# VectorE's order in the attention, two passes for the shared key, two transfers ahead of the experts, and unread products among the first turned rows, in one layer of a hybrid decoder

## What is computed

```
u = rmsnorm(h);  proj = u @ w_in        # c_q, c_kv, k_pe, hq, hf, hi, hg, gm, gh
o_mla = mla_branch(c_q, c_kv, k_pe)     # 8 heads, causal; k_pe: a rotary key of 32 columns, shared by all heads
o_hg  = hgrn2_branch(hq, hf, hi, hg)    # gated linear recurrence, chunkwise
merged = sigmoid(gm) * (o_mla @ w_br_mla) + sigmoid(gh) * (o_hg @ w_br_hgrn)
h = h + merged @ w_out
u = rmsnorm(h);  h = h + hier_moe(u)    # top group of 8, then top 2 of its 8 experts; 64 experts of width 256
return rmsnorm(h)[:, 16:]
```

## Time and profile before

| | us |
|---|---|
| median of 3 runs | 1494.26 |
| lowest and highest | 1493.94, 1495.15 |
| the profiled execution | 1496.1 |
| its span, first to last instruction | 1494.4 |
| TensorE busy | 1377.6 (92%) |
| VectorE, ScalarE busy | 581.8, 561.4 |
| mean granted TensorE clock | 0.980 |

### The profile page before, as it was taken

How to read it: one execution, slowest core, us unless ns; L and a number is a source line. 1 busy time by engine, 2 the same in 40 slices (tenths; PEclk the granted TensorE clock), 3 DMA queues, 4 the chain that set the end, 5 groups by cost and what they waited for, 6 DMA issues and landing times. The chain is left out here.

```text
span 1494.4 us, 21048 instructions
## 1 busy us (share of the span) xinstructions
PE 1377.6 (92%) x8471; PEld 983.6 (66%) x8471; DVE 581.8 (39%) x1303; ACT 561.4 (38%) x1066; POOL 101.6 (7%) x131
## 2 busy tenths in 40 slices
PE   5999999999999999999999999999987878688786
PEld 5888887787888887666667888855544444344442
DVE  6455565432531054656677556411110111111117
ACT  6534355222322146444552355533322222222223
POOL 0000000000000000000000011311111111111100
PEclk9999999999999999989999999999999999999998
DMA  6111111112234333112137654999999999999998
GB/s 185 43 29 43 29 29 43 30 32 78 80 97 122 101 89 124 57 36 71 36 120 240 253 194 157 321 416 415 415 416 416 416 417 416 416 416 417 415 403 333
DMA packets 130433, 312.53 MB, mean 209 GB/s; under 512 B 31120, under 2 KB 77200, under 8 KB 113184
## 3 DMA queue, kind: packets, MB, share of 16 engines
q1 hardware_dynamic: 118304, 285.96, 51.2%
q0 software_dynamic: 12032, 25.22, 4.4%
HBM read 283.81 MB, written 41.98 MB: 218 GB/s over the span
## 5 line engine op out<-in xcount | busy, mean ns | idle before, releaser
L2397 PE MATMUL ps<-r,m_xT 128*64 128x256 f32 x2048 | 253.4, 403 | 68.2 <-DMA r<-in_w 67.6
L130 PE MATMUL ps<-uTh,h_wh 128*128 128x512 f32 (+3 forms) x696 | 263.8, 379 | 4.4 <-DVE uTl L566 2.4
L131 PE MATMUL ps<-uTl,h_wh 128*128 128x512 f32 (+3 forms) x696 | 255.9, 368 | 0.0
L132 PE MATMUL ps<-uTh,h_wl 128*128 128x512 f32 (+3 forms) x696 | 255.6, 367 | 0.0
L2397 PEld LDWEIGHTS ps<-r,m_xT 128*64 128x64 f32 x2048 | 150.6, 145 | 153.5 <-DMA r<-in_w 76.1
L130 PEld LDWEIGHTS ps<-uTh,h_wh 128*128 128x128 f32 (+1 forms) x696 | 129.4, 186 | 28.7 <-DVE uTl L566 4.3
L2313 DVE TENSOR_TENSOR m_prod<-m_sig,ps 128x128 f32<-128x128 f32 x64 | 18.4, 288 | 333.4 <-ACT m_sig L2284 333.4
L132 PEld LDWEIGHTS ps<-uTh,h_wl 128*128 128x128 f32 (+1 forms) x696 | 129.3, 186 | 20.1
L131 PEld LDWEIGHTS ps<-uTl,h_wh 128*128 128x128 f32 (+1 forms) x696 | 129.6, 186 | 19.5 <-issue 0.2
L2379 PE MATMUL ps<-r,m_hT 128*64 128x512 f32 x512 | 122.4, 598 | 1.3 <-DVE m_hT L2317 0.9
L2274 ACT ACTIVATE m_y<-ps,gate 64x512 f32<-64x512 f32 x128 | 87.4, 682 | 80.0 <-PE ps L2379 78.4
(11 more groups left out here) (363 smaller groups left out, 2098.7 us busy)
## 6 DMA issues: line engine op xcount, KB each, us to landing
r<-in_w SPq DMA_DIRECT2D x190, 1024.0 KB, 24.3
h_w<-in_w_in SPq DMA_DIRECT2D x37, 512.0 KB, 4.3
gates<-h_sg POOLq DMA_DIRECT2D x16, 512.0 KB, 2.9
r<-y_moe SPq DMA_DIRECT2D x8, 1024.0 KB, 17.1
br_gate<-gates SPq DMA_DIRECT2D x14, 512.0 KB, 4.1
e_wo<-in_w_out SPq DMA_DIRECT2D x4, 1024.0 KB, 6.1
f_x<-in_x SPq DMA_DIRECT2D x8, 512.0 KB, 5.1
h_mid<-f_x SPq DMA_DIRECT2D x8, 512.0 KB, 4.5
```

Of the source, the lines that this page charges most:

```text
L130: pe.matmul(out, lh, rh, start=start, stop=False)
L131: pe.matmul(out, lh, rl, start=False, stop=False)
L132: return pe.matmul(out, ll, rh, start=False, stop=stop)
L2397: ins = pe.matmul(bank(UP_BANK + e % 2, 0, DE, CAP * f, CAP * (f + 1)).rearrange("p (r f) -> p r f", r=2), xT[i % 2][:, j, CAP * k:CAP * ( ...
```

## The change

- **Unread products.** A `keep_up` in the first stage puts 34 products of the identity with ones ahead of flip(0), then 6, 24 and 10 ahead of flips 1 to 3, and 12 behind flip(3), ahead of the first projection. They write bank 3, which nothing reads then.
- **Shared key.** The 32 columns of low weights are written beside the 32 of high weights, and a piece is 8 times two matmuls (high and low rows) with 64 weight columns in place of 8 times three with 32. Partitions 0 to 31 of the bank then hold the products with high weights, 32 to 63 those with low. ScalarE copies the first (counting `pp_ok`), VectorE adds the second (`summed_p`, counting `p_ok`).
- **Attention.** VectorE does peak(k+1,1) ahead of normed(k+1,0) in every step.
- **Transfers.** The last u is stored by ScalarE's queue, right behind its scaling and a wait for it, not by SyncE's; the first of expert 6's two upper transfers stands ahead of store_h(7) and of the wait for gathered rows.

```diff
@@ scalar, vector: the shared key
-                    act.activation(kpe[0:ROPE, c:c + m], bank(p % 3, 0, m, ROPE), ACT.Copy).then_inc(p_ok, 1)
+                    act.activation(kpe[0:ROPE, c:c + m], bank(p % 3, 0, m, ROPE), ACT.Copy).then_inc(pp_ok, 1)
...
-                dve.tensor_tensor(used(wl, J), used(w, J), used(wh, J).bitcast(F32), ALU.subtract).then_inc(wl_ok, 1)
+                low_part = wh[J % 2][:, :, ROPE:2 * ROPE] if JOBS[J][0] == "p" else used(wl, J)
+                dve.tensor_tensor(low_part, used(w, J), used(wh, J).bitcast(F32), ALU.subtract).then_inc(wl_ok, 1)
...
+            def summed_p(n):
+
+                c0, m = cols_of(LAT + 5)[n]
+                at_bank = spot[LAT + 5, n] % 3 * 512
+                dve.wait_ge(pp_ok, n + 1)
+                dve.tensor_tensor(kpe[0:ROPE, c0:c0 + m], kpe[0:ROPE, c0:c0 + m],
+                                  g.ps[ROPE:2 * ROPE, at_bank:at_bank + m], ALU.add).then_inc(p_ok, 1)
...
+                    if B == HG and s in (27, 29):
+                        summed_p(s // 2 - 13)
+            summed_p(2)
@@ tensor: the shared key
+                if JOBS[J][0] == "p":
+
+                    for j in range(4 * y, 4 * y + 4):
+                        for u_one in (g.uTh, g.uTl):
+                            last = pe.matmul(bank(p % 3, 0, m, 2 * ROPE), wh[J % 2][:, j, 0:2 * ROPE], u_one[:, j, col:col + m],
+                                             start=j == 0 and u_one is g.uTh, stop=j == DK - 1 and u_one is g.uTl)
+                for j in range(4 * y, 4 * y + 4) if JOBS[J][0] != "p" else ():
+                    last = mm3(pe, bank(p % 3, 0, m), wh[J % 2][:, j, :], wl[J % 2][:, j, :], g.uTh[:, j, col:col + m],
@@ tensor: the first turned rows
+            def keep_up(n):
+
+                for _ in range(n):
+                    pe.matmul(bank(RB, 0, P), g.ident[:, :], g.ones[:, :], start=True, stop=True)
+
             pe.wait_ge(consts, 4)
-            for n in range(4):
+            for n, unread in enumerate((34, 6, 24, 10)):
+                keep_up(unread)
                 flip(n)
+            keep_up(12)
@@ vector: the attention
-                if k + 2 == len(steps):
+                if more:
 
                     peak(k + 1, 1)
                     normed(k + 1, 0)
-                    normed(k + 1, 1)
-                elif more:
-                    normed(k + 1, 0)
-                    peak(k + 1, 1)
                     normed(k + 1, 1)
@@ sync and scalar: ahead of the experts
             sp.wait_ge(w_mm, 2 * TT)
-            store_u(TT - 1)
             g.load_down(sp, 4, 4)
             g.load_down(sp, 5, 5)
+            g.load_up(sp, 6, 6, (0,))
             store_h(TT - 1)
 
             sp.wait_ge(g.x_in[0], 16)
-            g.load_up(sp, 6, 6)
+            g.load_up(sp, 6, 6, (1,))
             g.load_down(sp, 6, 6)
...
                     act.activation(u[:, :], u[:, :], ACT.Copy, scale=sc[:, 14:15]).then_inc(u_ok, 1)
+                    act.wait_ge(u_ok, TT)
+                    act.dma_start(g.u2[t * P:(t + 1) * P, :], u[:, :]).then_inc(u_out, 16)
```

More of the change, by code:

```diff
@@ L211, in project_part @@
         sg_out = [sem(f"h_sg_out{b}") for b in range(2)]
+        pp_ok = sem("h_pp_ok")
         raw_ok, p_ok, ns_ok, ms_mm, nr_ok, n_ok, nh_ok, nl_ok = (
@@ L840, in half @@
                 col, m = cols_of(J)[n]
-                rows = ROPE if JOBS[J][0] == "p" else P
                 if cols_of(J) is REAL:
                     col += META
-                for j in range(4 * y, 4 * y + 4):
-                    last = mm3(pe, bank(p % 3, 0, m, rows), wh[J % 2][:, j, 0:rows], wl[J % 2][:, j, 0:rows], g.uTh[:, j, col:col + m],
+                if JOBS[J][0] == "p":
[5 more added lines that the diff above has]
+                    last = mm3(pe, bank(p % 3, 0, m), wh[J % 2][:, j, :], wl[J % 2][:, j, :], g.uTh[:, j, col:col + m],
                                g.uTl[:, j, col:col + m], j == 0, j == DK - 1)
@@ L1465, in expert_loaders, with load_up @@
     down = g.w2[0].rearrange("e (j p) n -> p e j n", j=2)
-    def load_up(eng, e, b):
-        for r in range(2):
+    def load_up(eng, e, b, parts=(0, 1)):
+        for r in parts:
             eng.dma_start(g.r13[b][:, r, :, :], up[r][:, bass.ds(e, 1), :, :].rearrange("p a j f -> p (a j) f")
```

## The result

| | before | changed | changed / before, 95% interval |
|---|---|---|---|
| median | 1494.66 | 1485.8 | 0.9941 (0.9923 to 0.996) |
| lowest and highest of 4 runs | 1493.94, 1495.15 | 1483.43, 1488.37 | |
| the profiled execution, its span | 1496.1, 1494.4 | 1488.4, 1486.6 | |

8.9 us are gone (6 to 11.5 by the interval of the ratio); 1486.2 was forecast. The sum held and two of its four terms did not: the attention gave 9 us where I had put 6, the transfers cost 2 us where I had put a gain of 1.5. That the sum still came out is luck: the errors cancel.

What follows compares the result with a forecast made beforehand. TensorE was taken to bound the kernel up to the routing, DMA in the experts. Unread products +3.2, shared key -3.8, attention -6.0 and transfers -1.5 sum to -8.1 us: from 1494.26 to 1486.2 us, range 1480.8 to 1493.6.

Steps and rivals of the forecast that it cites:

- The bound of each regime: Up to the routing TensorE sets the pace; in the experts the end follows DMA's bytes, and earlier savings pass on in full.
- Part 1: Start of the kernel: 86 unread calls delay the first projection to 26.1 us, less 1.4 for its warm clock: +3.2 us.
- the slow level ahead of the clock's rise: Kernel's start: work that begins slowly loses half the time until the clock rises, taken as 1.5 us.
- rival A: Unread products cost half or fit into existing waits, so the clock's gain stays: -2.8 in place of +3.2, 1480.2 us; chance 0.10.
- Part 2: Shared key: three pieces lose 8 matmuls each, 24 in all, and VectorE's additions lie in free slots: -3.8 us.
- Part 3: Attention: the new VectorE order removes most of TensorE's waits for normed rows: -6.0 us.
- all of them at best: Attention: of 8.3 us of waits 1.5 fall in the last step, so at most 6.8 us can be gained.
- head 0 pays 0.35: Attention: head 0's normed rows come later under the new order, so a stall of 0.35 us arises at turn(.,0).
- Part 4: Transfers around the routing: earlier loads close holes in DMA: -1.5 us, ends 0 and -3.
- the gain is 2.5 us less the gather's delay: Around the routing: a megabyte sent ahead gains 2.5 us less the gather's delay, which lies between 0 and 2.5.
- Rival B: Attention: TensorE waits for normed(.,0) in all steps, 7.0 us lost and no stall removed: 1499.2 us; chance 0.10.
- rival C: Stalls only move (-2.0 to -3.4), the gather is late (0), the clock slow to rise (+5.1): 1492.6 us; chance 0.15.

Runs made afterwards that it cites:

- e5: Changed kernel with SyncE storing u again ahead of the lower loads, expert 6's first upper megabyte still ahead: 1483.98 us, ratio 0.9925.
- e12: Same kernel as e10, but unread calls only ahead of the first two flips (17, 3, 0, 0 and none behind): 1479.22 us, ratio 0.9903.
- e4: Changed kernel with half the unread products, 43 calls (17, 3, 12, 5 and 6) in place of 86: 1477.94 us, ratio 0.9894.
- e7: Changed kernel with the old transfers put back and unread calls 20, 0, 9, 6 and 9: 1479.01 us, ratio 0.99.
- e2: Changed kernel without the 86 unread products: 1481.75 us, ratio 0.9909.
- e8: Kernel before with the shared key's two passes as the only change: 1490.15 us, ratio 0.9973.
- e3: Changed kernel with VectorE's old order in the attention: 1495.69 us, ratio 1.0002.
- e1: Changed kernel with the old transfers put back: SyncE stores u ahead of the lower loads, expert 6 behind the gathered rows: 1484.03 us, ratio 0.9928.
- e6: Changed kernel with expert 6 wholly behind the gathered rows, ScalarE still storing u: 1487.34 us, ratio 0.9955.
- e10: Changed kernel with half the unread products (17, 3, 12, 5 and 6 calls) and the old transfers put back: 1476.12 us, ratio 0.9878.
- e11: Same kernel as e10, but the lower loads of experts 4 and 5 (2 MB) moved behind the gathered rows: 1480.41 us, ratio 0.9912.

## Why the prediction was right, and where not

**The bound of each regime** held. What was gained ahead of the routing reached the last u (-10.4), and behind it the end followed DMA.

**Part 1, unread products: +3.2 said, +4.4 in the profile and +4.05 timed.** Two records a call at 0.112 us, 24.6 us for the sum of the calls and flips, TensorE as what is last, 1.4 us from the warm projection: all held. The mis-sized term is the slow level ahead of the clock's rise: I took 1.5 us and it was 27.37 - 24.6 = 2.8. It isn't a fixed price either: the row at 1.78 us is (10.38 - 0.27) - 67 x 0.112 = 2.6 us too long in the changed kernel and 2.2 in e5 with the same 34 calls, 2.7 in e12 and 1.9 in e4 with the same 17, and 1.5 in e7 with 20, always from the same start. What sets it stays open; the 1.5 us that I took is the lowest of them. The rule of the Trainium skill (TensorE: Matmul & The Clock Gate, section Why this matters for your kernels) to keep TensorE busy to get past the slow level isn't wrong for that: e4 gains 2 to 4 us by it over e2, the changed kernel loses 4 with twice the calls. What decides is whether the calls fit into the time in which nothing else is ready; rival A had the right place ("TensorE idles 8.49 us") and the wrong count.

**Part 2, shared key: -3.8 said, -3.8 and -3.9 (e8).**

**Part 3, attention: -6.0 said, -9.3 at equal clock.** The mechanism is as told. The step that failed is the bound "all of them at best", 6.8 us: I took the recorded idle time for all that a stall costs. (The bound was misread, too: 0.83 + 0.34 = 1.2 us of the 8.3 fall in the last step, not 1.5, so 7.1 were to be had.) Taking half of the low level's time off each, the new order gives 404.1 to 404.5 us from the sums to the merge in all ten profiled kernels that have it, the old order 413.3, 413.9 and 413.6 (before, e3, e8): 9.3 us (9.5 between kernels with equally many low stretches), while the recorded idle time fell by 8.3 - 1.2 = 7.1. About 0.2 us for each of ten stalls doesn't stand in the waits; block 3 shows 0.89 for 0.73. The rows of block 3 show where the rest is: idle is counted from the modelled end of the last matmul, and without a stall TensorE goes on before that end. In the changed kernel turn(.,1) starts 697.99 - 696.91 = 1.08 us after the scores, whose row lasts 1.25: an overlap of 0.17 us, and 0.73 + 0.17 is the 0.89, to a hundredth. For the other nine stalls this is argued by analogy. The step "head 0 pays 0.35" failed too: its turn(.,0) has no stall in any block but the last. And 1.7 us more of the profile's difference is the clock (1.4 with the 9.5 us), which was no term of the sum.

**Part 4, transfers: -1.5 said, +1.8 timed.** The failed step is "the gain is 2.5 us less the gather's delay". Three things are wrong in it. A megabyte sent ahead isn't gained where the buffers are full anyway: the hole moves to 970 us (e5 beside e1: to 968). The delay is not the gather's own (4.00 us, shorter than the 7.08 of the earlier trace rows) but that of the store that the gather waits for: u was written behind 3 MB of weights asked for 4 us before, 9.57 us in place of 5.2. And a queue of ScalarE's own is no way past them: the Trainium skill, DMA: Bandwidth & Descriptors, section Issuing engines are not separate DMA queues, says that transfers of all issuing engines interleave on the same 16 engines. I had cited it for "worth nothing" and not gone on to what it interleaves with; e6 agrees with it, at 8.37 us. In SyncE's list store_u stood ahead of the loads, and that order, I take it, was the protection; a store by SyncE behind the loads would have shown it.

**The sum.** +4.4 - 3.8 - 9.3 - 1.7 + 2.6 = -7.8 us, the difference of the spans. My -8.1 came out near it because its errors cancel: 1.2 too little for the unread products and 4.1 too much gain for the transfers stand against 3.3 too little gain in the attention and 1.7 of the clock (-8.1 + 1.2 + 4.1 - 3.3 - 1.7 = -7.8). By the medians the four parts are +4.05 (e2), -3.9 (e8), -9.9 (e3) and +1.8 us (e1), together -7.95 against -8.9 measured, within the intervals. Rival B's stalls and rival C's "stalls only move" are refuted by the waits and e3; C's late gather was true.

## To carry to other kernels

Unread products pay only in time in which the engine has nothing else to do: count them (records, at the slow pace until the clock is up) against the pause, part by part; 43 calls gained 2 to 4 us where 86 lost 4. A store that a gather waits for belongs ahead of the bulk loads in the order of asking (5.2 us against 8.4 to 9.6 behind them); whether the other queue had a part in it these runs don't say. And where an in-order engine stalls in mid-stream, a stall can be worth more than the waits show (here some 0.2 us each), so the recorded idle time is no upper bound of what its removal gives.

## What was not expected of the hardware

- In the attention the low level of the clock comes in stretches of 3.4 us (or two or three of them on end), some 1.5 us lost for each where TensorE is the bound. Where they fall isn't tied to the part of the program: the merge, behind a pause of 2.5 us, starts slow in before, e3, e4, e7 and e10 and at full clock in the changed kernel, e1, e2, e5, e6, e8, e11 and e12, with both orders of VectorE on either side. Kernels that differ in an early part differ by up to 3 us this way later on (404.5 against 407.5 in the attention); what sets their place stays open.
- In the first 25 us of the kernel before, the column of granted clock shows 1.00 while the flips of full tiles take 1.94 to 1.97 us; e12's flip at 16.09 takes the same 1.97 us with 0.50 in the column. There the durations tell the level more surely than the column.
